# Gate projections of the second block as seven products of halves, and the rotary angles moved behind the token shift

## The reference

```
proj = h @ w_in                       # qa ka va qb kb vb fl qc kc vc qi ki wi gl
br_a, br_b, br_c = three attentions of 8 heads (stick-breaking, forgetting, sparse)
gates = sigmoid(gl.reshape(b, s, 3, 1024))
y = gates[0] * (br_a @ w_branch[0]) + gates[1] * (br_b @ w_branch[1]) + gates[2] * (br_c @ w_branch[2])
x = x + y @ w_out
x = x + square(relu(rmsnorm(x) @ w_up)) @ w_down
```

## Time and profile before

| | us |
|---|---|
| median of three runs | 1619.41 |
| lowest, highest | 1618.2, 1623.53 |
| the profiled execution | 1617.27 |
| its span, first to last instruction | 1615.4 |
| busy: PE, PEld, DVE, ACT, POOL | 1543.3, 1335.0, 745.7, 335.7, 164.8 |

### The profile page before, as it was taken

One profiled execution on the slowest core, in us unless ns is written; L12 is line 12 of the kernel. 1 busy time (PEld: TensorE's weight loads), 2 busy tenths in 40 slices (PEclk: granted clock), 3 DMA queues, 4 the chain that ended last, 5 costly groups with the idle time before them and its releaser, 6 DMA issues.

```text
span 1615.4 us, 30716 instructions
## 1 busy us (share of the span) xinstructions
PE 1543.3 (96%) x13507; PEld 1335.0 (83%) x13507; DVE 745.7 (46%) x1408; ACT 335.7 (21%) x713; POOL 164.8 (10%) x97
## 2 busy tenths in 40 slices
PE   7799999899799899999999999999999999999998
PEld 2566858688688688987788999998998878899998
DVE  2741244555743326633431766521753433186643
ACT  1201042533423311033400121000103340012000
POOL 3403001000000025400000000004540000000000
PEclk9899999999899999999999999999999999999999
DMA  9213240000003534423244444463443323444551
GB/s 361 96 52 104 79 157 3 3 2 3 18 4 106 132 105 157 157 104 111 110 146 157 156 157 157 172 169 106 157 157 117 129 112 113 155 157 157 176 185 45
DMA packets 110901, 191.59 MB, mean 119 GB/s; under 512 B 20888, under 2 KB 27296, under 8 KB 110640
## 3 DMA queue, kind: packets, MB, share of 16 engines
q1 hardware_dynamic: 109776, 188.29, 34.1%
q0 software_dynamic: 960, 1.33, 0.3%
q10 hardware_dynamic: 32, 0.01, 0.0%
HBM read 188.57 MB, written 1.05 MB: 117 GB/s over the span
## 4 chain that ended last, share of the span: by engine, by line
PE 85%; DVE 4%; PEld 3%; DMA 2%; ACT 2%; issue 2%; DVEq 1%; PEldq 1%; ACTq 1%; SPq 0%
PE psum L1341 22%; PE psum L1175 12%; PE psum L1278 10%; PE psum L1205 6%; PE psum L897 6%; PE psum L822 4%; PE psum L1201 3%; PEld psum L1470 2%; PE psum L1386 2%; PE psum L1451 2%; PE psum L1470 2%; PE psum L1058 2%; PE psum L1490 1%; PE psum L1264 1%; PE psum L1309 1%
## 5 line engine op out<-in xcount | busy, mean ns | idle before, releaser
L1341 PEld LDWEIGHTS psum<-arena 128*128 128x128 f32 x3136 | 350.5, 192 | 0.1
L1341 PE MATMUL psum<-arena 128*128 128x128 f32 x3136 | 350.5, 274 | 0.0
L1899 ACT ACTIVATE arena<-psum 128x512 f32<-128x512 f32 (+6 forms) x226 | 111.6, 500 | 614.0 <-PE psum L1341 176.7
L1175 PE MATMUL psum<-arena 128*128 128x256 f32 x928 | 202.6, 379 | 0.0
L1175 PEld LDWEIGHTS psum<-arena 128*128 128x128 f32 x928 | 175.3, 189 | 25.6 <-issue 0.3
L1278 PE MATMUL psum<-arena 128*128 128x256 f32 x768 | 176.5, 382 | 0.0
L1278 PEld LDWEIGHTS psum<-arena 128*128 128x128 f32 x768 | 141.8, 189 | 26.6 <-issue 5.3
L1205 PEld LDWEIGHTS psum<-arena 128*128 128x128 f32 x896 | 100.7, 192 | 0.2
L1205 PE MATMUL psum<-arena 128*128 128x128 f32 x896 | 100.7, 274 | 0.0
L897 PEld LDWEIGHTS psum<-arena 64*64 64x64 f32 x3072 | 92.3, 134 | 6.8 <-issue 4.6
L897 PE MATMUL psum<-arena 64*64 64x64 f32 x3072 | 96.1, 219 | 1.6 <-issue 1.6
(11 more groups left out here) (382 smaller groups left out, 1846.3 us busy)
## 6 DMA issues: line engine op xcount, KB each, us to landing
arena<-in_w_in SPq DMA_DIRECT2D x33, 2048.0 KB, 8.3
arena<-in_w_up SPq DMA_DIRECT2D x16, 2048.0 KB, 8.5
arena<-in_w_down SPq DMA_DIRECT2D x16, 2048.0 KB, 7.9
arena<-in_w_out SPq DMA_DIRECT2D x6, 2048.0 KB, 7.8
arena<-in_w_branch SPq DMA_DIRECT2D x6, 2048.0 KB, 7.7
arena<-in_mod_w SPq DMA_DIRECT2D x5, 2048.0 KB, 14.4
arena<-in_w_in SPq DMA_DIRECT2D x3, 1024.0 KB, 7.2
arena<-in_w_in SPq DMA_DIRECT2D x12, 256.0 KB, 4.8
```

What stands on the lines that cost most here:

```text
L1175: mm = pe.matmul(b[:, i * T:(i + 1) * T], w[:, k, c:c + P], src[:, k, :], start=k == 0, stop=k == ks - 1)
L1341: mm = pe.matmul(b[:, n * P:(n + 1) * P], left[:, k, n * P:(n + 1) * P], right[:, k, :], start=first and n == 0 and k == 0, stop=last and ...
L1899: return act.activation(dst, src, ACT.Copy, scale=scale)
```

## The change

**Gates.** Each gate chunk becomes seven products of halves: 1, 6, 7 in its even step before the transposes and 5 behind them, 2, 3 and 4 likewise in the odd step (`GATE_STEPS`). `head_product` becomes `product_of_halves`, with its waits moved to the caller. Product 6 waits for GpSimd's first signal of the chunk, product 7 for the second. GpSimd makes six more sets of sums a layer behind the head sums. Their places are free one after the other: in `gt`, `br`, `sg` and a new spare tile; so each operation has the event of `gate_sums_after` ahead of it, and the last chunks wait for the weights of step 7 (`weights_ready` 8), since these sums take the place of A's sigmoids. Per chunk ScalarE copies product 1 and makes one Tanh over 4 x 256 columns, in place, one chunk later (`gates_out`), between the exponentials and the copy of wT. VectorE adds the products (`gate_added`) and now finishes pair i in its own step i, not in step i+1. The banks' plan and `CHUNK_ENDS` follow.

**Setup.** VectorE's `lbc` operations and the angles move into its first T turn, ScalarE's exponential and sines behind its fourth T turn. In `TAIL` the turn E2 comes before T11, and from there the T turns are one place later among the E and H turns.

```diff
-TAIL = "TTETETTTTTTTTTETETETEHTETEHTHTHTETHEH"
+TAIL = "TTETETTTTTTTTETTEETEHTETEHTHTHTETHTEH"
...
+GATE_STEPS = (((1, 6, 7), (5,)), ((2, 3), (4,)))
...
             p += [(f"z{i}", "A" if PAIRS[i][0] == "A" else "D", 2)]
+            p += [(f"gl{i // 2}_{m}", "A" if m == 1 else "D", 1) for m in GATE_STEPS[i % 2][0]]
...
-            p += [(f"gl{i}", "A", 1)]
+            p += [(f"gl{i // 2}_{m}", "D", 1) for m in GATE_STEPS[i % 2][1]]
...
+        gate_sums = [(in_gt[1], in_gt[2], in_br[0]), (in_gt[3], in_gt[4], in_gt[5]), (in_br[0], in_br[2], in_gt[3]),
+                     (in_gt[4], in_gt[5], in_br[2]), (in_gt[5], in_spare, in_sg[0]), (in_sg[1], in_spare, in_sg[0])]
+        gate_sums_after = [("kb_4", "kb_4", "kb_4"), ("vb_4", "vb_4", "vb_4"), ("gl0_3", "gl0_3", "gl1_5"),
+                           ("gl1_6", "gl1_3", "gl2_6"), ("gl3_6", None, None), (None, "gl4_6", "gl4_3")]
...
+                    for c in range(GATES):
+                        n = len(FIRST) + 9 + c
+                        gp.wait_ge(s_slot[SLOT[n]], l * SLOT_PER_LAYER[SLOT[n]] + landed(n))
+                        if c == GATES - 1:
+                            gp.wait_ge(sem("weights_ready"), l * len(PAIRS) + 8)
...
+                        if after1:
+                            ly.wait_filled(gp, after1, l)
+                        gp.tensor_tensor(s1, w21, w22, ALU.add)
+                        gp.drain()
+                        if after2:
+                            ly.wait_filled(gp, after2, l)
+                        gp.tensor_tensor(s2, s1, w11, ALU.subtract)
+                        gp.drain().then_inc(sem("gate_weights_summed"), 1)
+                        if c == GATES - 2:
+                            gp.wait_ge(sem("weights_ready"), l * len(PAIRS) + 8)
+                        gp.tensor_tensor(w21, w11, w21, ALU.subtract)
+                        if after4:
+                            ly.wait_filled(gp, after4, l)
+                        gp.tensor_tensor(s4, w12, s2, ALU.subtract)
+                        gp.drain().then_inc(sem("gate_weights_summed"), 1)
...
+                def gate_products(ms):
+                    for m in ms:
+                        b = take_bank(ly, f"gl{i // 2}_{m}", l)
+                        if m in (6, 7):
+                            pe.wait_ge(sem("gate_weights_summed"), 2 * (GATES * l + i // 2) + (1 if m == 6 else 2))
+                        product_of_halves(b, w, m, gate_sums[i // 2]).then_inc(ly.filled, 1)
...
-            for i in range(len(PAIRS) + 1):
-                if i < len(PAIRS) and PAIRS[i][0] != "A":
+            for i in range(len(PAIRS)):
+                if PAIRS[i][0] != "A":
                     masked(i)
-                if i:
-                    finish(i - 1)
+                gate_added(i // 2, GATE_STEPS[i % 2][0])
+                finish(i)
+                gate_added(i // 2, GATE_STEPS[i % 2][1])
```

More of the change, by code:

```diff
@@ L512, in build @@
         tok_first = take(4 * 4 * T, (4, 4, T))
+        half = KT // 2
         top[0] = base
@@ L531, in build @@
         work0 = top[0]
-        zm, pp, wgt, wt, sg = [take(2 * 2 * 384, (2, 2, 384)) for _ in range(5)]
+        zm, pp, wgt, wt = [take(2 * 2 * 384, (2, 2, 384)) for _ in range(4)]
+        sg_at = top[0]
+        (sg,) = [take(2 * 2 * 384, (2, 2, 384)) for _ in range(1)]
         rdots = pp.rearrange("p s h t -> p (s h) t")
@@ L545, in build @@
         cosr, sinr = wk[:, 0:T], bias_c[:, 0:T]
+        spare_sum = take(half * T)
+        rot_t = spare_sum[:, 0:512]
         top_attn = top[0]
@@ L1272, in layer_tensor @@
                         w = use_chunk(pe, n0 + 9 + i // 2, l)
[L1273 to L1279, removed]
+                def gate_products(ms):
[4 more added lines that the diff above has]
+                        product_of_halves(b, w, m, gate_sums[i // 2]).then_inc(ly.filled, 1)
                 if i < last:
-                    gate_tile(0, 0, KT)
-                    gate_tile(1, 0, KT // 2)
+                    gate_products(GATE_STEPS[i % 2][0])
                 if i:
@@ L1672, in values_out, with first_gates, gates_out @@
                 emptied(ly, copy(br[:, "ABC".index(kind), p, :], bank(ly, f"o{i}", l)[:, 0:T]))
+            def first_gates(c):
+                ly.wait_filled(act, f"gl{c}_1", l)
+                emptied(ly, copy(gt[:, 4 * c:4 * c + 2, 0:P], blocks_of(bank(ly, f"gl{c}_1", l)[:, 0:T])))
+            def gates_out(c):
+                act.wait_ge(sem("gates_added"), GATES * l + c + 1)
+                v = gt[:, 4 * c:4 * c + 4, :]
+                act.activation(v, v, ACT.Tanh, scale=0.5)
             last = len(PAIRS)
@@ L1692, in layer_scalar @@
                         done("exps_ready")
+                if i and i % 2 == 0 and i < last:
+                    gates_out(i // 2 - 1)
                 if i:
                     weights_out(i - 1)
[L1695 to L1699, removed]
+                if i == last:
+                    gates_out(GATES - 1)
                 if i:
@@ L1936, in _ @@
                     emptied(xp, ins)
[L1938 to L1941, removed]
                 act.wait_ge(sem("shifted"), 1)
@@ L1961, in tail_scalar @@
                         yield
+                    act.wait_ge(sem("lb_shifted"), 1)
+                    act.activation(lbw, lbw, ACT.Exp)
+                    done("lb_exp")
+                    angles()
                     for _ in range(8):
@@ L2143, in tail_vector @@
             def tail_vector():
+                lg = cols[:, COL["hgrn_lb_logits"]:COL["hgrn_lb_logits"] + 6]
+                dve.tensor_tensor(lbw, lg, lg, ALU.subtract)
+                done("lb_shifted")
+                dve.wait_ge(sem("lb_exp"), 1)
+                dve.reciprocal(omlb, lbw)
+                fence()
+                dve.tensor_tensor(lbw, lbw, omlb, ALU.mult)
+                fence()
+                dve.tensor_tensor(lbw, lbw, lbw, ALU.subtract)
+                fence()
+                dve.tensor_scalar(lbc[:, :, 0:1], lbw.unsqueeze(2), 0.0, None, ALU.max)
+                fence()
+                dve.tensor_scalar(lbc[:, :, 1:2], lbc[:, :, 0:1], -1.0, 1.0, ALU.mult, ALU.add)
+                angles_vector(dve, done, fence)
                 for _ in range(7):
```

79 lines of the change are left out of this document (52 added, 27 removed).

## The result

| kernel | median, us | lowest, highest | ratio to before, 95% interval |
|---|---|---|---|
| before | 1621.47 (4 runs) | 1618.2, 1623.67 | |
| changed | 1598.93 (4 runs) | 1596.14, 1600.96 | 0.9854 [0.9833, 0.9874] |

The change is faster by 22.5 us between the medians (1.46% by the ratio, between 1.26 and 1.67%). Forecast were 1609 and a range of 1599 to 1618: the direction is right, the gain is twice as large as forecast (10.3), and the time lies at the lower edge of the range, 0.07 us outside. The profiled execution took 1600.96 us around its span of 1598.9.

What follows compares the result with a forecast made beforehand. TensorE, carrying 85% of the 1615.4 us span, was taken as the bound. Two layers -2.6, setup -6.7 and order -1.0 made -10.3: 1607.0 from the profiled 1617.27, or 1609 as median of runs; range 1599 to 1618.

Steps and rivals of the forecast that it cites:

- gates, TensorE alone: Attention gates: seven products of halves take 12.51 us a chunk instead of 13.60, gaining 6.5 us a layer.
- step 8's wait for the weights: Attention, step 8: the 1.76 us wait for step 7's weights goes because finish comes earlier, -1.8 us a layer.
- product 7 waits for GpSimd: Attention, step 8: chunk 4's last two sums come late, a new TensorE wait of 2.6 to 3.4, taken as 3.4 us.
- collisions: Attention, steps 2, 3 and 9: VectorE's finishes block behind GpSimd's sums, weights' copies end late, +3.6 us a layer.
- Setup: First project groups: with the angles behind the shift, TensorE's 6.71 us wait at 75.18 goes entirely, -6.7 us.
- Order of turns: Setup's tail: the new order of turns addresses TensorE's 2.19 us wait for VectorE at 235.84; -1.0 us, bounds -3 and +2.
- Rival (1): Attention: no collisions, sums fall in VectorE's gaps; -5.7 us a layer, -19.1 in all, 1600 us; chance 0.20.
- Rival (3): Attention: the port binds, all 12 steps lose 1.3 us; +9.9 a layer, +12.1 in all, 1631 us; chance 0.09.

Runs made afterwards that it cites:

- the kernel without sums: Changed kernel with GpSimd's gate sums left out, products reading plain weight quarters, so other gates are computed: 1590.24 us, 0.9792.
- angles alone: Kernel before with only the lower bounds and angles moved behind the shift, turns as before: 1617.34 us, 0.9962.
- product 5 first: Changed kernel with chunk 4's products in the order 1, 6, 5 | 7 instead of 1, 6, 7 | 5: 1600.14 us, 0.9863.
- old order: Changed kernel with the order of turns in the tail put back to that of the kernel before: 1603.6 us, 0.9882.
- gates alone: Kernel before with the new gates, their sums and the new place of finish; angles and turns as before: 1613.13 us, 0.9934.
- five sums: Changed kernel with each gate chunk's first sum made twice by GpSimd, five operations in place of four: 1609.52 us, 0.9912.
- later wait for chunk 4: Changed kernel; of chunk 4's two last sums only the last waits for the weights of step 7: 1596.35 us, 0.9833.

## Why the prediction was wrong, step by step

Per layer, in us:

| term | forecast | measured | by |
|---|---|---|---|
| gates, TensorE alone | -6.5 | -8.2 | the kernel without sums, less the next row |
| step 8's wait for the weights | -1.8 | -2.0 | before: step 8 takes 11.43, the other A and C steps 9.45 |
| product 7 waits for GpSimd | +3.4 | +2.65 | timeline after |
| collisions | +3.6 | 0 | all other steps alike with and without sums |
| half clock behind the wait | not in the sum | +1.9 | stretches after |
| sum | -1.3 | -5.7 | stage 119.24 to 113.52 |

The step of the prediction that failed is the collision term: 3.6 us a layer for delays of VectorE that TensorE never waited for. TensorE's own gain was put 1.7 too small, and the half clock behind waits was not in the sum at all.

- **Setup: right, too small.** The wait went and nothing took its place, in the places and times forecast (68.71 for 68.47; the angles at 138 to 144). The reason given for the angles' length holds too: the two operations of 4.60 us in the earlier trace rows take 0.67 at 140.72, where GpSimd is idle. What the sum missed is that the same edit takes a clock fall away: 1.67 us. The clock was in the trace of before: I priced the wait by its length, and read no stretches behind it.
- **Order of turns.** Forecast -1.0 for a wait of 2.19 that did go. In the two profiles it gave 1.7, of which 1.4 were lost again where a clock fall lasted longer, so that just -0.3 is left in the ledger. Where the setup's wait is gone in both orders, the order gives 6.9 us (angles alone) and 4.0 us (changed kernel) between the medians, of which the wait is 2.2. Right in sign, too small.
- **Gates on TensorE.** The account by starts of loads was nearer than busy time (1.09 and 2.12 us a chunk; measured 1.37). Its error: for the new steps I put 2.78 us (0.76 + 2.02) from the transposes' first load to the values, with what the old groups spend beside their own loads. It is 2.65 there (742.21 to 744.86), and odd and even steps take 7.87 and 9.66 instead of 8.01 and 9.80. Twelve steps at 0.14 are the missing 1.7.
- **Product 7.** The one wait in step 8 came as forecast, at the lower of my two values, since the collisions in steps 6 and 7 didn't hold the finish up.
- **Collisions: the failed step.** They happen (mean 629 ns for 317; groups of four TENSOR_SCALARs take up to 4.34 us for 1.01). The step: "masked(2) then starts some 2 us late, the exponentials and Tanh of step 2 too, and the weights' copy ends 1.3 us late for TensorE", and twice more. TensorE waited for the copy in none of them. The delay forecast at 2 us was 1, and the room forecast at 0.7 (2 less 1.3) was 1.7: 0.84 from the Tanh to the end of the transposes, and 0.87 from the copy to the values. With one sum more a chunk TensorE does wait for the copy, but in step 1, which the forecast didn't name.
- **Rival (1)** named the stage, 5.7 less a layer, and so the total, 1600. Its reason, that sums fall in VectorE's gaps, is wrong. Its figure is right by luck, by two errors that cancel: 1.7 + 0.2 more from TensorE and 1.9 lost to the clock.
- **Rival (3)**: a slower kernel appears with three sums more a chunk, by 0.8%, and by a few long waits, not by 1.3 us in each step.

The Trainium skill (SBUF — State Buffer, Who interferes with whom) was borne out: in the changed kernel's stage no TENSOR_TENSOR with a PSUM operand was longer than 0.43 us, while TENSOR_SCALARs and products of two SBUF inputs took up to 2.39 and 2.75. The rule tells which operations are late and not whether anybody waits for them; I used it for the second.

## What to carry to other kernels

Price a collision by the room of who waits for its result, not by the operation's own delay; that room is best measured by a kernel that leaves the disturbing work out and one that adds to it. Read the granted clock behind each wait that an edit removes or adds: here the setup's wait was worth 1.7 us more than its length and the added one cost 1.9 more, while behind the two shorter ones of the kernel before the clock stayed full. When a wait is moved, look for what it had been covering.

## What the hardware showed that was not expected

- **A wait's price goes on behind it.** Behind idle times of TensorE of 6.71 (before), 2.65 (after), 3.03 (product 5 first) and 2.18 us (old order) the granted clock was 0.50 for some 3 to 10 us, at a cost of 1.7, 1.9, 1.6 and 4.4 us. Behind 1.76 (before, step 8), behind 2.19 in the kernel before and in the gates alone, and behind 2.3 (five sums, step 1) it stayed at 1.00. The same wait of 2.19 was followed by a fall in both traces in which the setup's wait was gone, and by none in both in which it was there, so its length alone doesn't decide. Why is open. The Trainium skill (TensorE: Matmul & The Clock Gate, Part 1: The HAM clock gate) has two states, 1.2 and 2.4 GHz, and the rows agree: every row shows 1.00, 0.50, or a mean of a stretch that contains a change.
- **Falls that no edit explains.** In the second block 16 products (`fl`) behind 32 narrow ones took 5.35 us in the changed kernel's first layer:

```profile
593.68 3.63 PE L1224 MATMUL psum<-arena 128*128 128x4 f32 x32
597.16 5.35 PE L1259 MATMUL psum<-arena 128*72 128x256 f32 x16
```

In the kernel before the same 16 took 3.67 us in the first layer and 5.35 in the second, with a mean clock of 0.67. The stretch that holds them (second block's first product to the first scores) took 109.5 us in the changed kernel's profile and 107.8 in its repetition. In the 14 traces of this case it took 107.8 us five times, 109.5 four times and 111.1 five times. In the same kernel it comes and goes, 1.7 us a time; what decides is open.
- **Short VectorE operations pass together.** Four TENSOR_SCALARs that met back-to-back sums took 2.4 to 4.4 us in the changed kernel, and 4.62 in the later wait for chunk 4, not four times a sum of 2.0 to 2.4: one ends late with a sum, and the next passes before the following sum holds one up.
